# An fp32 transformer kernel: x and the first weights on one DMA queue in the order of use, constants behind them

## The reference

```python
for l in range(2):
    x = x + 0.5 * swiglu_ffn(x, ffn1_norm[l], ffn1_w_gate[l], ffn1_w_up[l], ffn1_w_down[l])
    h = rms_norm(x, mix_norm[l])
    ...   # w_in, three mixers (differential, chunked, retention), branch and output projections
    x = x + 0.5 * swiglu_ffn(x, ffn2_norm[l], ffn2_w_gate[l], ffn2_w_up[l], ffn2_w_down[l])
...       # second block: norm, three mixers, output projection, swiglu, final norm

def swiglu_ffn(x, norm, w_gate, w_up, w_down):
    h = rms_norm(x, norm)
    return (jax.nn.silu(h @ w_gate) * (h @ w_up)) @ w_down
```

## Time and profile before

| what | value |
|---|---|
| median of 3 runs | 3420.56 us (3419.51 to 3420.67) |
| span of the profiled execution | 3420.8 us |
| PE busy | 3363.2 us (98%) |
| PEld busy | 2601.9 us (76%) |
| DVE busy | 1746.2 us (51%) |
| ACT busy | 1255.8 us (37%) |
| first matmul starts | 18.50 us |

### The profile page before, as it was taken

How to read it: one execution, slowest core, us unless ns; L and a number is a source line. 1 busy time by engine, 2 the same in 40 slices (tenths; PEclk the granted TensorE clock), 3 DMA queues, 4 the chain that set the end, 5 groups by cost and what they waited for, 6 DMA issues and landing times.

```text
span 3420.8 us, 35895 instructions
## 1 busy us (share of the span) xinstructions
PE 3363.2 (98%) x14282; PEld 2601.9 (76%) x14282; DVE 1746.2 (51%) x2858; ACT 1255.8 (37%) x1891; POOL 28.6 (1%) x57
## 2 busy tenths in 40 slices
PE   7999999999999999999999999999999998999998
PEld 6888866577788888888876666888888756878886
DVE  6333687635463335433487744455334557884333
ACT  4222446424243233322355533334223346343232
POOL 0000000000000000000000000000000100000000
PEclk9999999999999999999999999999999999999999
DMA  4333321222223332333321222323332533323332
GB/s 140 102 95 90 94 73 53 71 80 77 93 87 105 93 95 90 105 99 95 96 85 51 71 64 78 92 92 94 99 93 87 109 61 50 84 80 99 98 91 70
DMA packets 282071, 297.66 MB, mean 87 GB/s; under 512 B 9776, under 2 KB 270256, under 8 KB 281904
## 3 DMA queue, kind: packets, MB, share of 16 engines
q1 hardware_dynamic: 277408, 283.15, 28.9%
q0 software_dynamic: 3536, 10.55, 1.0%
q10 hardware_dynamic: 960, 1.67, 0.1%
HBM read 293.24 MB, written 2.10 MB: 86 GB/s over the span
## 4 chain that ended last, share of the span: by engine, by line
PE 91%; DVE 5%; ACT 2%; issue 1%; DMA 0%; DVEq 0%; SPq 0%; ACTq 0%
PE bank L218 90%; ACT k_sc L214 1%; PE bank L224 1%; DVE k_wl L170 1%; DVE k_sc L180 1%; DVE k_sc L196 0%; DMA k_raw<-in_ffn_w_gate 0%; ACT L208 0%; DVE k_sc L170 0%; DVE k_x L180 0%; ACT k_wh L214 0%; DVE k_xc L180 0%; DVE k_xl L170 0%; DVE k_cv L180 0%; DVE k_ul L170 0%
## 5 line engine op out<-in xcount | busy, mean ns | idle before, releaser
L170 DVE TENSOR_TENSOR k_wl<-k_raw,k_wh 128x1024 fp32r<-128x1024 f32 x545 | 654.6, 1204 | 1178.6 <-ACT k_wh L214 1178.4
L218 PE MATMUL bank<-k_xh,k_wh 128*128 128x512 f32 x2376 | 960.7, 404 | 5.0 <-ACT k_wh L214 3.3
L218 PE MATMUL bank<-k_xh,k_wl 128*128 128x512 f32 x2376 | 928.9, 391 | 4.7 <-DVE k_wl L170 4.7
L218 PE MATMUL bank<-k_xl,k_wh 128*128 128x512 f32 x2376 | 928.4, 391 | 1.7 <-DVE k_xl L170 1.7
L214 ACT ACTIVATE k_wh<-k_raw 128x1024 fp32r<-128x1024 f32 x545 | 563.9, 1039 | 990.3 <-PE bank L218 721.6
L218 PEld LDWEIGHTS bank<-k_xh,k_wh 128*128 128x128 f32 x2376 | 447.2, 188 | 164.1 <-issue 67.9
L218 PEld LDWEIGHTS bank<-k_xh,k_wl 128*128 128x128 f32 x2376 | 447.5, 188 | 100.3 <-DVE k_wl L170 5.5
L218 PEld LDWEIGHTS bank<-k_xl,k_wh 128*128 128x128 f32 x2376 | 447.8, 188 | 96.7 <-issue 8.1
L218 PE MATMUL bank<-k_uh,k_wh 128*128 128x512 f32 x512 | 206.2, 403 | 18.6 <-ACT k_uh L214 18.5
L218 PE MATMUL bank<-k_Ga,k_wh 128*128 128x512 f32 x704 | 218.2, 391 | 0.0
L218 PE MATMUL bank<-k_Gb,k_wh 128*128 128x512 f32 x704 | 218.2, 391 | 0.0
(11 more groups left out here) (278 smaller groups left out, 3687.9 us busy)
## 6 DMA issues: line engine op xcount, KB each, us to landing
k_raw<-in_w_in SPq DMA_DIRECT2D x153, 512.0 KB, 3.7
k_raw<-in_ffn_w_gate SPq DMA_DIRECT2D x88, 512.0 KB, 3.8
k_raw<-in_ffn_w_up SPq DMA_DIRECT2D x88, 512.0 KB, 3.8
k_raw<-in_ffn_w_down SPq DMA_DIRECT2D x80, 512.0 KB, 3.4
k_raw<-in_w_out SPq DMA_DIRECT2D x28, 512.0 KB, 3.4
k_raw<-in_w_gate SPq DMA_DIRECT2D x22, 512.0 KB, 3.8
k_raw<-in_w_up SPq DMA_DIRECT2D x22, 512.0 KB, 3.8
k_raw<-in_w_down SPq DMA_DIRECT2D x20, 512.0 KB, 3.4
```

The lines of the kernel that those rows point to most:

```text
L170: return q.op(lambda e: e.tensor_tensor(out, a, b, op), cost(out))
L218: fn = lambda e: e.matmul(out, l, r, start=start, stop=stop, skip_group_check=True)
```

## The change

Four edits. `chunk` records only the split of the piece that is asked for, for the first four pieces. The very first product (`wg`, first column pair) uses pieces of 2 k-tiles, 128x512 elements or 256 KB, so that it has four of them. x is loaded in eight tiles of 256 KB, each with its own semaphore, all by SP, and interleaved with the four weight pieces by a table `after_dma`. GpSimd waits for the last x tile before it loads the constants.

```diff
-        while self.next_split < min(len(self.plan), i + SPLIT if i else 2):
+        while self.next_split < min(len(self.plan), i + SPLIT if i > 3 else i + 1):
...
         self.S.run(lambda e: e.dma_start(dst, src).then_inc(sem, 16))
+        for load in self.after_dma.pop(i, []):
+            load()
...
-                self.linear(wg, l, 0, KD, c, 256, act, dgate)
+                self.linear(wg, l, 0, KD, c, 256, act, dgate, 1, 2 if base == "a0" and c == 0 else KC)
...
-        for i in range(4):
-            sem = self.xsem[i]
-            (self.A if i else self.S).run(lambda e, i=i, sem=sem: e.dma_start(X3[:, 2 * i:2 * i + 2, :], xs[:, 2 * i:2 * i + 2, :]).then_inc(sem, 16))
+        def xload(k):
+            sem = self.xsem[k]
+            return lambda: self.S.run(lambda e: e.dma_start(X3[:, k:k + 1, :], xs[:, k:k + 1, :]).then_inc(sem, 16))
+
+        xl = [xload(k) for k in range(8)]
+        xl[0]()
+        self.after_dma = {0: xl[1:3], 1: xl[3:5], 2: xl[5:7], 3: xl[7:8]}
+        self.G.wait([("x7", self.xsem[7], 16)])
         self.load(C[:, :], self.d["cpack"])
         self.load(lamt[:, :], self.d["lampack"])
...
-        self.xtok = [(f"x{k // 2}", self.xsem[k // 2], 16) for k in range(8)]
+        self.xtok = [(f"x{k}", self.xsem[k], 16) for k in range(8)]
```

More of the change, by code:

```diff
@@ L1481, in build @@
         self.nsq, self.acc_free, self.acc_tok, self.r_free = 0, [], None, []
-        self.xsem = [self.mksem(f"s_x{i}") for i in range(4)]
+        self.xsem = [self.mksem(f"s_x{i}") for i in range(8)]
         self.vsem = self.mksem("s_vec")
```

## The result

The changed kernel takes **3427.9 us** (median of 13 runs, 3426.38 to 3431.39) against 3420.17 us of the kernel before in the same session (13 runs, 3419.51 to 3424.77): ratio 1.0023, 95% interval 1.0015 to 1.0031. That is 7.7 us slower, where 3.9 were forecast. The profiled execution took 3427.93, its span is 3426.1.

The account below looks back on a forecast made before the run. TensorE, busy 98%, was taken as the bound, so only its first 18.5 us counted. The later up product (+2.6) and low clock (+1.3) gave +3.9 on 3420.6, 3424.5 us; range 3421 to 3428.

Parts of the forecast that it names:

- the low clock: TensorE after the 8 us wait: slow matmuls at 1.2 GHz, charged 1.3 us, bounds 0 and 1.8.
- Transfers, first matmul: Kernel start: last x tile lands near 12.4, first matmul at 7.5 in place of 18.5, 11.0 us earlier.
- c0: First quarter of the gate pair, 12 matmuls; forecast to land at 4.9 and be done on TensorE by 12.1.
- rival 3: Start transfers: 12 smaller DMAs on one queue run well below 350 GB/s; slower than 0.2%, 3427.8 at 230 GB/s; chance 9%.
- c1: Second quarter of the gate pair: its split done at 15.2, TensorE waiting 3.2 us for it.
- The order, c4: First up piece, split behind norm and silus: TensorE waits 8 us, third up matmul at 35.2, 2.6 us later.
- Constants nought: Constants loaded after the last x tile land at 22.2, just before first use; cost nought, up to 1 us.
- c1 to c3: Second to fourth quarters of the gate pair; low clock there allowed only -0.2/+0.3 us in the range.
- Span against median: Starting point: profiled span 3420.8 and median 3420.56 us can be taken as one.
- the chain's own: Chain through norm and silus to the up product: 2.6 us later in equal work, before any clock loss.
- Rival 2: Kernel start: quicker norm chain, TensorE loses only the gate-pair waits and about half of the 8 us; near 3416; chance 5%.

Follow-up runs that it names:

- e8_warm_after: The changed kernel with 18 matmuls on a tile of ones, into an unread bank, ahead of its first matmul; 3426.51 us.
- e9_early_and_warm: The changed kernel with the first two up-piece splits recorded ahead of the norm and 18 matmuls on ones ahead of its first matmul; 3416.05 us.
- e1_up_splits_early: The changed kernel with the splits of the first two up pieces recorded ahead of table load, norm and silus; 3415.98 us.
- e10_fill_both_waits: The changed kernel with unread matmuls in both TensorE waits, 8 after the first gate piece and 32 between gate and up product; 3424.06 us.
- e4_transfers_only: The kernel before with only the new transfers (x in eight loads on SP, constants behind the last); old 512 KB pieces and split rule; 3416.05 us.
- after_again: The changed kernel run again without any edit, in another session; 3427.2 us.
- e6_warm_before: The kernel before with 61 matmuls on a tile of ones, into an unread bank, ahead of its first matmul; 3421.32 us.
- e2: The changed kernel with 32 unread matmuls between the gate and the up product, filling the long wait only; 3425.47 us.
- e5: The kernel before with only the four small gate pieces and the changed split rule, its transfers kept; 3429.29 us.
- e7_old_rule_warm: The changed kernel with the split rule of before and 29 matmuls on a tile of ones ahead of its first matmul; 3414.01 us.

## Why the prediction was wrong

It put 86% on "within 0.2%"; the time is 0.23% above before. The range ended at 3428, 7.4 above the 3420.6 it started from; measured are 7.7 above before in the same session, where 3.9 were forecast. That 3427.9 itself still lies below 3428 is luck: before ran 0.4 faster there. The mechanism was right; what failed is the size of one term, the low clock. The steps one by one:

- **Transfers, first matmul.** 7.5 forecast, 7.44 measured; c0's split at 4.80 (4.9 forecast, with 0.4 for the completion that no row shows). Right, and rival 3 (slow small DMAs) is dead: the rates are 313 to 404 GB/s from 2.5 to 12 us, with 256 KB pieces, and x7 has landed by 12.63, when GpSimd goes on (12.4 forecast). ("No row here has 256 KB" overlooks `k_lamv` in the earlier trace rows, which shared the engines and says little of the rate.)
- **c1.** Split done 15.2 forecast; PE went on at 15.16. The wait was 2.03 and not 3.2, because all 12 matmuls of c0 ran at the 0.43 pace and not 7 as in before. Missing that did next to no harm, for they lay in front of a wait (e8_warm_after, 0.7 us; e9_early_and_warm, none).
- **The order, c4.** A wait of 8 us for k_wh, with two silus just ahead of it on ACT, then none: measured 7.74, silus at 32.09, no wait up to 90. The third matmul of the up pair at 35.2; measured 35.57. Right, and e1_up_splits_early shows the cause. In part 35.2 was luck: with the waits filled (e10_fill_both_waits) the same matmul ran at 34.71, so the chain was put too late by some 0.3 to 0.5, and the low clock ahead of it, charged with 0.2, made that good.
- **Constants nought.** Right: no wait for them, and e4_transfers_only with them behind x7 is faster than before.
- **The low clock, the step that failed.** One stretch was charged, 1.3 us with 1.8 as its upper end, and c1 to c3 only as -0.2/+0.3. There were two that cost. Behind the wait of 2.03 the slow matmuls put the ones matmul 0.87 late (0.17 of it is c1's split), and with it norm, silus and c4. Behind the wait of 7.74 the slow stretch went on to 40.85, longer than the one at before's start: the 12 steps from 35.57 took 5.28 us instead of 12 x 0.228 = 2.74, 2.5 us. Together 3.2 to 3.4 us; e10_fill_both_waits measures 14 matmuls, 3.2 (10, 2.3 us, against after_again). The bound of 1.8 came from one stretch of eight steps and was taken for a limit. With 3.2 in place of 1.3 and the chain's own 2.3 in place of 2.6 the sum is +5.5, what the trace shows.
- **Span against median.** "Span 3420.8 against the median 3420.56, so the two can be taken as one." They can't. Time less span is 1.8 us in the profiled executions (3427.93 and 3426.1; 3422.92 and 3421.1 in e6_warm_before), so before's profiled execution stood for 3422.6, 2.4 above the median of 3420.17. Differences taken inside its start are not touched by that; but it shows that single executions of one kernel differ by more than the sum was meant to resolve.
- **What stays open.** The traces show 5.3 to 5.5, the medians 7.7; in the second session it is 4.6 and 6.0. Part of it is before: 3420.17 is its lowest median of four sessions, and against the other three 3427.9 is 6.6 to 7.2 more. Part is the place near 940 us and the one near 2265: the traced execution of before had the low clock at both and stood 2.4 above its median, the traced one of after had it at both and stood at its median. Whether the change makes these stretches likelier isn't shown by one trace of before and two of after; 1 to 2 us are not placed.

Rival 2 ("part is kept, near 3416") named a time that the transfers do reach, but with splits ahead of the norm, not with a quicker norm.

## What to carry over

On an in-order engine, ask of each piece of work moved earlier what now stands behind it: here one number in the rule for splits decided between 3415 and 3427 us, and the earlier first matmul was worth nothing while the up product's split stood behind the norm. Charge every new TensorE wait with the slow matmuls that follow it as well (7 to 14 of them behind the waits of 2 us and more here), and count them only where no other wait comes next: in front of a wait, or under a slower feeder, a slow matmul costs little or nothing (taking them away won 0.7 us in e8_warm_after, within the spread, and nothing in e9_early_and_warm and e6_warm_before). And read the profiled execution against the spread of the medians before a forecast is made to microseconds.

## What the hardware showed unexpectedly

The length of the slow stretch isn't a fixed price. Behind waits of 2.0 to 4.0 us (after, after_again, e1, e2, e5, e8, e9) 7 to 13 matmuls were slow, behind those of 7.75 us (after, after_again, e5, e8) 14, 11, 12 and 10; at 0.2 us each that is 1.4 to 2.8 us, with no order by the length of the wait. Short waits are no safe ground either: behind the 1.23 us of e7_old_rule_warm and the 1.50 of e6_warm_before none was slow, but behind the pair of 0.81 and 0.83 us near 940 us 7 or 8 were, in eight executions of 13. Nor does the low clock begin with the wait: in after it is granted from near 17 us on, some 2 us after PE went on at 15.16, and before the second stretch it fell while PE stood still (1.00 from 26.5 to 30, 0.58 from 30 to 34.2). Matmuls that nobody reads, put in the wait, took the stretch away (e2, e10), and the kernel with 40 matmuls more was 3 us faster.
